# Twenty weight slots for the experts instead of sixteen: constants parted by their life, the normed buffer as a slot

## The reference, cut to what matters

```python
x  = first_block(...)                                   # two layers, RMS norms, feed-forward
h  = rms_norm(x, norm_mix_2);  p = h @ w_in_2           # RWKV, pool, attention, gates
x  = x + (sum of gated branches) @ w_out_2
h  = rms_norm(x, norm_ffn_2)
aff = softmax(h @ router)                               # 256 tokens x 16 experts
for e in experts:                                       # each takes the 32 tokens with the highest affinity
    xe = h[chosen]                                      # 32 x 1024
    ye = (silu(xe @ gate[e]) * (xe @ up[e])) @ down[e]  # three 1024 x 1024 matrices
    x[chosen] += aff[chosen, e] * ye
out = rms_norm(x, norm_final_2)
```

## Time and profile before

| | us |
|---|---|
| median of 3 runs (lowest, highest) | 1851.73 (1849.95, 1852.37) |
| the profiled execution, whole | 1851.07 |
| its span, first to last instruction | 1849.3 |
| PE busy in it | 1551.8 (84%) |
| DMA in the chain that ended last | 25% of the span |
| mean granted PE clock, as a share of full | 0.918 |

### The profile page before, as it was taken

How to read it: one execution, slowest core, us unless ns; L and a number is a source line. 1 busy time by engine, 2 the same in 40 slices (tenths; PEclk the granted TensorE clock), 3 DMA queues, 4 the chain that set the end, 5 groups by cost and what they waited for, 6 DMA issues and landing times.

```text
span 1849.3 us, 25541 instructions
## 1 busy us (share of the span) xinstructions
PE 1551.8 (84%) x11252; PEld 1156.7 (63%) x11252; DVE 539.2 (29%) x1181; ACT 263.1 (14%) x634; POOL 72.1 (4%) x96
## 2 busy tenths in 40 slices
PE   7979999998968999999878778999888666676664
PEld 4857788886736888887756556777774323232221
DVE  3671444402032311005564674422321000000001
ACT  2331100002122100001222232222010000000001
POOL 0230000000000000000011000300000000000000
PEclk8999999998969999999989899999999877878778
DMA  8466577744334544433300000232559999999997
GB/s 369 158 248 271 197 301 298 293 162 153 143 116 158 228 149 147 160 136 117 133 25 2 24 24 2 91 114 91 212 205 404 419 420 420 420 419 420 420 420 291
DMA packets 57630, 405.93 MB, mean 220 GB/s; under 512 B 6184, under 2 KB 8360, under 8 KB 9008
## 3 DMA queue, kind: packets, MB, share of 16 engines
q1 hardware_dynamic: 53696, 388.26, 53.5%
q10 hardware_dynamic: 3824, 16.04, 2.2%
HBM read 403.21 MB, written 1.06 MB: 219 GB/s over the span
## 4 chain that ended last, share of the span: by engine, by line
PE 63%; DMA 25%; DVE 8%; ACT 2%; issue 1%; SPq 0%; POOL 0%; ACTq 0%; DVEq 0%
PE bank L437 62%; DMA weight_ring<-weights 14%; DMA arena<-weights 11%; DVE arena L1567 3%; DVE arena L1573 2%; PE bank L444 1%; ACT arena L1200 1%; DVE arena L1570 1%; DVE arena L1898 1%; DVE rstd L1623 0%; DMA arena<-x 0%; DVE rstd L1965 0%; DVE arena L1760 0%; DVE arena L1896 0%; ACT normed_T L1200 0%
## 5 line engine op out<-in xcount | busy, mean ns | idle before, releaser
L437 PE MATMUL bank<-normed_T,weight_ring 128*128 128x256 f32 x2640 | 607.2, 387 | 27.1 <-ACT arena L1200 12.4
L437 PEld LDWEIGHTS bank<-normed_T,weight_ring 128*128 128x128 f32 x2640 | 503.1, 193 | 108.4 <-ACT arena L1200 18.1
L437 PE MATMUL bank<-arena 64*64 64x64 f32 (+5 forms) x4592 | 340.4, 335 | 82.6 <-DMA arena<-weights 54.0
L437 PEld LDWEIGHTS bank<-arena 64*64 64x64 f32 (+5 forms) x4592 | 223.1, 148 | 207.7 <-DMA arena<-weights 80.3
L437 PE MATMUL bank<-arena,weight_ring 128*128 128x256 f32 x1456 | 329.7, 384 | 9.7 <-ACT arena L1200 6.8
L437 PEld LDWEIGHTS bank<-arena,weight_ring 128*128 128x128 f32 x1456 | 278.3, 192 | 51.0 <-issue 8.5
L1200 ACT ACTIVATE arena<-bank 128x256 f32<-128x256 f32 (+4 forms) x305 | 111.8, 374 | 1130.2 <-PE bank L437 761.7
L1573 DVE SCALAR_TENSOR_TENSOR arena<-arena,bank 128x256 f32<-128x256 f32 x141 | 59.4, 421 | 532.0 <-PE bank L437 275.7
L437 PE MATMUL bank<-weight_ring,arena 128*32 128x256 f32 (+1 forms) x1184 | 108.4, 464 | 61.8 <-DMA weight_ring<-weights 59.7
L437 PEld LDWEIGHTS bank<-weight_ring,arena 128*32 128x32 f32 (+1 forms) x1184 | 41.7, 127 | 123.4 <-DMA weight_ring<-weights 86.0
L444 PE MATMUL bank<-packed_consts,arena 128*128 128x128 f32 (+1 forms) x166 | 42.0, 353 | 61.4 <-DVE arena L1570 27.8
(11 more groups left out here) (130 smaller groups left out, 648.4 us busy)
## 6 DMA issues: line engine op xcount, KB each, us to landing
weight_ring<-weights SPq DMA_DIRECT2D x258, 1024.0 KB, 6.2
arena<-weights SPq DMA_DIRECT2D x88, 1024.0 KB, 27.3
packed_consts<-weights SPq DMA_DIRECT2D x22, 1024.0 KB, 26.4
arena<-weights ACTq DMA_DIRECT2D x8, 1024.0 KB, 18.4
packed_consts<-packed ACTq DMA_DIRECT2D x1, 2848.0 KB
arena<-bias_by_distance ACTq DMA_DIRECT2D x2, 1024.0 KB, 6.9
packed_consts<-weights ACTq DMA_DIRECT2D x2, 1024.0 KB, 35.1
arena<-x SPq DMA_DIRECT2D x1, 1024.0 KB, 5.2
```

Source lines behind the costliest of these rows:

```text
L437: return e.matmul(out, lhsT, rhs, start=start, stop=stop, skip_group_check=True)
```

## The change

- The slots for experts become 20: 14 outside the ring (`EXTRA` = 9 + 3 + 2) and the 6 of the ring. By turn: 0 to 8 are free when the ten were (`AHEAD` = 9); 9 to 11 lie over what the branches use (`BEHIND_BRANCH`); 12 to 17 are the ring; 18 lies over the merged branches, which `w_out_2` reads, and 19 is `hT_` (`BEHIND_W_OUT`).
- ACT issues 14 loads instead of 10: nine at the old place, three more behind a new wait for the last merged branch (`merged`), one behind the eight squares, one behind the four copies to `htok`. SP issues turns 12 to 17 and all from chunk 20 on.
- The constants are parted: 256 late columns stay in `packed_consts`, 5440 columns (`passing`) move to the end of the arena, where slots lie over them later. The late load is now two DMAs.
- `silu_c_copies`, `modulation_rows` and `rstd` become one buffer, in which `final_gain` is loaded; `y_stat` gets a buffer of its own.
- To make room for semaphores, the two of `bias_in` become one (the first attention step waits for both loads), and four of the RWKV's last norm become one, `ln_sum`, counted in the order in which PE raises them.

```diff
-IN_ARENA, IN_CONSTS = 8, 2
-AHEAD = IN_ARENA + IN_CONSTS
+AHEAD = 9
+BEHIND_BRANCH, BEHIND_W_OUT = 3, 2
+EXTRA = AHEAD + BEHIND_BRANCH + BEHIND_W_OUT
...
-        turn = (c - FIRST_EXPERT) % (AHEAD + SLOTS)
+        turn = (c - FIRST_EXPERT) % (EXTRA + SLOTS)
         if c < FIRST_EXPERT:
             slot = c % SLOTS
-        elif turn < AHEAD:
+        elif turn < AHEAD + BEHIND_BRANCH:
             slot = SLOTS + turn
+        elif turn < AHEAD + BEHIND_BRANCH + SLOTS:
+            slot = (FIRST_EXPERT + turn - AHEAD - BEHIND_BRANCH) % SLOTS
         else:
-            slot = (FIRST_EXPERT + turn - AHEAD) % SLOTS
+            slot = turn
...
-    e.dma_start(m.pk[:, EARLY_COLS:NCOLS], dram["packed"][:, EARLY_COLS:NCOLS]).then_inc(s.late, 16)
+    e.dma_start(m.pk[:, EARLY_COLS:KEPT_COLS], dram["packed"][:, EARLY_COLS:KEPT_COLS]).then_inc(s.late, 16)
+    e.dma_start(m.passing, dram["packed"][:, KEPT_COLS:NCOLS]).then_inc(s.late, 16)
...
     e.wait_ge(s.branch_sum, 2 * KD)
     e.wait_ge(s.o_out, 2 * n_items)
-    for c in range(FIRST_EXPERT, FIRST_EXPERT + AHEAD):
-        slot = PLACES[c][0]
-        e.dma_start(m.slots[slot], dram["weights"][c]).then_inc(s.filled[slot], 16)
+
+    def load(*turns):
+        for turn in turns:
+            slot = PLACES[FIRST_EXPERT + turn][0]
+            e.dma_start(m.slots[slot], dram["weights"][FIRST_EXPERT + turn]).then_inc(s.filled[slot], 16)
+
+    load(*range(AHEAD))
+    e.wait_ge(s.merged, KD)
+    load(*range(AHEAD, AHEAD + BEHIND_BRANCH))
     for n in range(KD):
         e.wait_ge(s.xT, 8 * NORM_FFN2 + n + 1)
         act(m.sq8[:, n * T:(n + 1) * T], xT[:, n, :], ACT.Square).then_inc(s.square, 1)
         if n == 0:
             e.preload_act_table(ACT.Sqrt)
+    load(AHEAD + BEHIND_BRANCH + SLOTS)
...
             act(m.htok[:, j, q * 512:(q + 1) * 512], B[2 * j + q][:, :], ACT.Copy, scale=m.st[:, j:j + 1]).then_inc(s.h_tok, 1)
+    load(AHEAD + BEHIND_BRANCH + SLOTS + 1)
...
-            if hd == 0:
-                e.wait_ge(s.bias_in[j], 16)
+            if i == 0:
+                e.wait_ge(s.bias_in, 16 * NT)
...
-        if FIRST_EXPERT <= c < FIRST_EXPERT + AHEAD:
+        if c >= FIRST_EXPERT and c < FIRST_EXPERT + EXTRA + SLOTS and slot >= SLOTS:
             continue
```

More of the change, by code:

```diff
@@ L76, in columns @@
         ("a0", 2 * KR), ("k_k", KR), ("k_a", KR), ("r_k", KR), ("ln_w", KR), ("ln_b", KR), ("pool_scale", KR),
-        ("q_norm", 1), ("k_norm", 1), ("norm_ffn_2", KD), ("rel_bias", HEADS),
+        ("q_norm", 1), ("k_norm", 1), ("norm_ffn_2", KD), ("rel_bias", HEADS), ("router", KD * EXPERTS), ("iota", CAP),
+    ]
+    passing = [
         ("w2", RW), ("a2", RW), ("g2", RW), ("pool_w", 4 * P), ("cos", T), ("sin", T), ("inv_cnt", 4 * T), ("onehot", 2 * T),
-        ("router", KD * EXPERTS), ("iota", CAP), ("blk", P), ("pair", P), ("half", P),
+        ("blk", P), ("pair", P), ("half", P),
         ("strict", 2 * P), ("incl", 2 * P), ("level", LEVELS * HALF), ("eye", HALF),
@@ L82, in columns @@
     at, out = 0, {}
-    for name, n in early + late:
+    for name, n in early + late + passing:
         out[name] = (at, n)
         at += n
-    return out, at, sum(n for _, n in early)
-COLS, NCOLS, EARLY_COLS = columns()
+    return out, at, sum(n for _, n in early), sum(n for _, n in early + late)
+COLS, NCOLS, EARLY_COLS, KEPT_COLS = columns()
 NTILES = (112 * KD + 20 * KD + LRU_HEADS * 8 + KD * KL + 2 * (2 * KF * KD + KD * KF) + 2 * KV_HEADS * KD + HEADS * KD
@@ L179 @@
 REL = {"sum": 1, "row": 2}
-LATE = {"consts": 16, "bias_out": 32, "final_gain": 48}
+LATE = {"consts": 32, "bias_out": 48, "final_gain": 64}
+LN_SUM = {"mean": 1, "var": 2, "bonus": 3, "g": 4}
 ROUTE_PE = {"sum": 2, "aff": 3, "place": 4}
@@ L194, in __init__ @@
             "consts", "late", "x_in", "stored", "freed", "freed_v")]
-        self.bias_in = [sem(f"bias_in{j}") for j in range(NT)]
-        self.filled = [sem(f"filled{j}") for j in range(SLOTS + AHEAD)]
+        self.bias_in = sem("bias_in")
+        self.filled = [sem(f"filled{j}") for j in range(SLOTS + EXTRA)]
         self.v_link, self.a_link, self.g_link, self.zeroed = [sem(n) for n in ("v_link", "a_link", "g_link", "zeroed")]
@@ L230, in __init__ @@
         (self.gram_c, self.masked_c, self.r_sum, self.r_out, self.u_sum, self.u_out, self.s_sum, self.state, self.y_sum, self.y_out,
-         self.mean_sum, self.y_sq, self.var_sum, self.bonus_in, self.bonus_sum, self.bonus, self.ln_root, self.g_sum, self.rwkv_out) = [sem(n) for n in (
+         self.ln_sum, self.y_sq, self.bonus_in, self.bonus, self.ln_root, self.rwkv_out) = [sem(n) for n in (
             "gram_c", "masked_c", "r_sum", "r_out", "u_sum", "u_out", "s_sum", "state", "y_sum", "y_out",
-            "mean_sum", "y_sq", "var_sum", "bonus_in", "bonus_sum", "bonus", "ln_root", "g_sum", "rwkv_out")]
+            "ln_sum", "y_sq", "bonus_in", "bonus", "ln_root", "rwkv_out")]
         (self.qk_pe, self.qk_v, self.qk_a, self.pooled, self.pool_sum, self.yb, self.merged) = [sem(n) for n in (
@@ L269, in __init__ @@
         self.ring = sbuf("weight_ring", SLOTS * TPC * P)
-        self.pk = sbuf("packed_consts", NCOLS)
+        self.pk = sbuf("packed_consts", KEPT_COLS)
         self.xT_ = sbuf("residual_T", KD * T)
@@ L275, in __init__ @@
         self.silu_c = sbuf("silu_c", KD)
-        self.silu32 = sbuf("silu_c_copies", 32 * KD)
-        self.mod_rows = sbuf("modulation_rows", 512)
-        self.rstd = sbuf("rstd", T)
+        rows = sbuf("silu_c_copies_modulation_rows_rstd", D)
+        self.silu32, self.mod_rows, self.rstd, self.final_gain = rows[:, 0:T], rows[:, T:3 * T], rows[:, 3 * T:4 * T], rows[:, :]
+        self.y_stat = sbuf("sums_of_the_last_norm", 5 * NT)
         self.rstd_x = sbuf("rstd_of_the_residual", T)
         n = (nc.sbuf_bytes_remaining // 4 - 64) if not callable(nc.sbuf_bytes_remaining) else nc.sbuf_bytes_remaining() // 4 - 64
+        whole = sbuf("arena", n)
+        self.passing = whole[:, n - (NCOLS - KEPT_COLS):n]
+        n_slot = TPC * P
+        ends = [n - j * n_slot for j in range(EXTRA)]
+        n -= NCOLS - KEPT_COLS
         self.n = n
-        self.area = area = sbuf("arena", n)
+        self.area = area = whole
         self.B = [ctx.enter_context(nc.psum_tensor(f"bank{b}", [P, 512], F32)) for b in range(8)]
@@ L338, in __init__ @@
         self.gates = [a.take(T), self.mod_rows[:, 0:T], self.mod_rows[:, T:2 * T], self.silu32[:, :], self.stage[0][:, 0:T], self.stage[1][:, 0:T]]
-        self.ahead_at = a.at - T - IN_ARENA * TPC * P
         assert a.at <= n - 2 * TW
+        gate0 = a.at - T
         for j in range(24 - N_EARLY):
@@ L343, in __init__ @@
         keep += (24 - N_EARLY) * T
-        n_slot = TPC * P
-        consts = COLS["w2"][0]
         self.slots = [self.ring[:, j * n_slot:(j + 1) * n_slot] for j in range(SLOTS)]
-        self.slots += [area[:, self.ahead_at + j * n_slot:self.ahead_at + (j + 1) * n_slot] for j in range(IN_ARENA)]
-        self.slots += [self.pk[:, consts + j * n_slot:consts + (j + 1) * n_slot] for j in range(IN_CONSTS)]
-        assert consts + IN_CONSTS * n_slot == COLS["router"][0]
+        at = [end - n_slot for end in ends[:-1]]
+        free = [x for x in at if x >= n or x + n_slot <= gate0 and x >= keep + (KD + 2) * T]
+        last = [x for x in at if x < keep + KD * T]
+        branch = [x for x in at if x not in free + last]
+        assert (len(free), len(branch), len(last)) == (AHEAD, BEHIND_BRANCH, BEHIND_W_OUT - 1), (free, branch, last)
+        self.slots += [whole[:, x:x + n_slot] for x in free + branch + last] + [self.hT_[:, :]]
+        self.experts_end = min(at)
         a = Arena(area, n, keep)
@@ L361, in __init__ @@
         self.pbuf2, self.ptb2, self.stat2 = [[a.take(k) for _ in range(NBUF)] for k in (T, NT * P, 4)]
-        a = Arena(self.hT_, KD * T)
-        self.final_gain, self.y_stat = a.take(D), a.take(5 * NT)
         self.yg = self.xT_
@@ L377, in __init__ @@
         self.zeros = a.take(P)
-        assert a.at <= self.ahead_at
+        assert a.at <= self.experts_end
         a = Arena(area, n, a.at)
@@ L382, in __init__ @@
         self.act_, self.hid_e, self.hidT, self.ye, self.comb = [a.take(T) for _ in range(5)]
-        assert a.at <= self.ahead_at
+        assert a.at <= self.experts_end
     def col(self, name, j=0, n=1):
         a = COLS[name][0] + j
+        if a >= KEPT_COLS:
+            return self.passing[:, a - KEPT_COLS:a - KEPT_COLS + n]
         return self.pk[:, a:a + n]
@@ L885, in finish @@
         e.wait_ge(s.y_out, 4 * ct + 4)
-        mm(B[4][:, 0:T], m.blk, m.yaT[:, ct * T:(ct + 1) * T], True, True).then_inc(s.mean_sum, 1)
+        mm(B[4][:, 0:T], m.blk, m.yaT[:, ct * T:(ct + 1) * T], True, True).then_inc(s.ln_sum, 1)
         yield
         e.wait_ge(s.y_sq, ct + 1)
-        mm(B[4][:, 0:T], m.blk, m.y2, True, True).then_inc(s.var_sum, 1)
+        mm(B[4][:, 0:T], m.blk, m.y2, True, True).then_inc(s.ln_sum, 1)
         e.wait_ge(s.bonus_in, ct + 1)
```

(14 more changed lines are left out.)

## The result

The changed kernel took 1842.02 us in the median of five runs (1838.19 to 1843.18), beside 1851.37 us (1849.59 to 1852.37) for the kernel before: ratio 0.9943, 95% interval 0.993 to 0.9957. Beside other kernels, on chips of their own sessions, it was measured twice more: 0.9945 (0.9933 to 0.9957) and 0.9937 (0.9922 to 0.9951). The forecast was 1841.6 us. Between these two medians lie 9.4 us.

The account below looks back on a forecast made before the run. The kernel's end was taken as bound by a constant-rate weight stream starting at the first freed slot. Four chunks at 2.517 us save 10.1 us, other parts zero: 1851.73 - 10.1 = 1841.6 us, forecast range 1840.0 to 1843.2.

Parts of the forecast that it names:

- The four slots: Expert weight stream: 19 chunks loaded ahead instead of 15, each worth 2.517 us; gain 10.1 us, bounds 10.0 and 10.2.
- The room in the gap: Idle DMA stretch before the experts, 1364.9 to 1386.0 us: all four added loads in before 1386 us, 6 us to spare.
- some 2 MB: Sign to check: the strip's slice around 1364 to 1386 us, before the experts, carries some 2 MB more.
- Turn 19: ACT's load behind the last copy to htok, starting at 1374.4 us, landed by some 1380 us.
- ACT's issues: ACT behind the merged wait: three issues, 1.5 us, done at 1337.1 us before the first square at 1338.5; cost nothing.
- The rival of a queue that blocks: ACT's three issues behind merged blocked 6.58 us each, PE standing 14.1 us: 1855.7 us; chance 0.05.
- Late constants, semaphores, addresses: Split late load bounded by 2 us gain or loss, taken as zero; merged semaphores and moved buffers cost nothing.
- The end: Last 16 matmuls take 1.07 us in full clock, 1.93 in half: 0 to +0.9 us, 1 us allowed in all.
- The check points: Last landing 1827.4 us instead of 1837.5; stream rate stays 420 GB/s; first waited landing later than 1412 us.

Follow-up runs that it names:

- another megabyte: Changed kernel with the 0.5 MB final_gain load done twice more, before the first expert; 1838.98 us beside 1838.43 for the changed kernel, ratio 0.9938 to the kernel before.
- Sixteen slots: Changed kernel with four slots taken away, all its other parts kept; 1849.59 us beside 1850.69 for the kernel before, ratio 0.9994.
- the kernel with two late slots: Changed kernel, all twenty slots, but turns 18 and 19 loaded only beside final_gain, as the first expert is about to start; ratio 0.9964 to the kernel before.
- pair of zeros and the freed slot: Changed kernel with the last w_out_2 slot freed in route_sums and two matmuls of zeros per late chunk of the last expert; ratio 0.9945 to the kernel before.
- eighteen: Changed kernel without ACT's two late routing loads (turns 18 and 19); ratio 0.9973 to the kernel before, stream 446.5 us.

## Why the prediction was right

*The four slots.* Foretold 10.1 us; the stream fell by 10.3 us in the first profile, and by 9.9 us from sixteen to twenty slots (451.2 to 441.3). The pace in the changed kernel is (1826.82 - 1428.73) / 158 chunks = 2.520 us, against 2.517 before. From the two kernels between, a stored chunk is worth (451.2 - 446.5) / 2 = 2.35 us and (446.5 - 441.3) / 2 = 2.6 us. By the share of HBM that "DMA: Bandwidth & Descriptors" of the Trainium skill gives (section "Bandwidth") it would be 2.9 us. The prediction set that share against the measurement without its condition: the same section gives it for two cores of a pair that both stream, and 425 GB/s for loads of 16 MB by a core alone. The runs, with one core at work, show 420 GB/s, so they are against the share and not against the page.

*The room in the gap.* Right: 150 GB/s in it, and with another megabyte in it still no cost. The gap carried 3.1 MB more and not "some 2 MB": of the two chunks more that were to pass ahead of it, only one had by 1364.6 us, and the other ran on until 1367 us, where the prediction itself has the queues run empty. Turn 19 came at 1371.0 us and not at 1374.4 us. That issue stands 0.6 us ahead of the four copies that precede it in the program (1371.65 us), as turn 18's stands at the start of the eighth square and not at its end. The step was too cautious.

*ACT's issues.* Right: 0.33 to 0.72 us each, the three behind the merge done at 1336.6 us (forecast 1337.1), and the first square didn't wait. The rival of a queue that blocks didn't come true.

*Late constants, semaphores, addresses.* Taken at zero with 2 us to either side. Sixteen slots with all of them gave 0.9994 (0.9985 to 1.0003), so zero stands, with 2.8 us at most of a gain. In the first profile the stage around 124 us stood 1.9 us later than before, which looked like a loss; by 568 us it was gone. The profiles scatter here anyway: one landmark, a table load on ACT, stands at 565.07 us in the kernel with two late slots, at 568.35 us before, at 568.11 us in the changed kernel and at 570.49 us with the pair of zeros and the freed slot, while from there to the table load of the routing these four take 801.5 to 801.7 us. In order: before, changed, two filled late, pair of zeros and freed slot:

```profile
568.35 1.28 ACT L1223 ACT_TABLE_LOAD   x1
1369.97 1.28 ACT L1512 ACT_TABLE_LOAD   x1
```

```profile
568.11 1.28 ACT L1237 ACT_TABLE_LOAD   x1
1369.66 1.28 ACT L1534 ACT_TABLE_LOAD   x1
```

```profile
565.07 1.28 ACT L1237 ACT_TABLE_LOAD   x1
1366.70 1.28 ACT L1533 ACT_TABLE_LOAD   x1
```

```profile
570.49 1.28 ACT L1244 ACT_TABLE_LOAD   x1
1372.13 1.28 ACT L1541 ACT_TABLE_LOAD   x1
```

*The end.* I named the right thing and sized it too small: 0.9 us for the last 16 matmuls, 1 us in all. It is 1.8 us, since the second group of 16 is slower too (2.11 against 1.17 us). In the profiled run this is why the span fell by 8.9 us and not by 10.1 us; that the median came out within 0.4 us of the forecast has some luck in it: the medians differ by 9.4 us and not by 10.1, and the forecast started from a median before of 1851.73 us where the kernel before, timed beside the changed one, had 1851.37 us.

*The check points.* The last landing was forecast for 1827.4 us and came at 1826.8 us; the rate stayed at 420 GB/s; the first waited landing moved from 1412 to 1428.7 us.

## What to carry to other kernels

Where a kernel ends in a stream at the rate of its DMA engines, its end is the time of the first load of the stream plus the bytes still to come: look for a stretch ahead of it in which the engines are idle, count the chunks that could be stored there, and each is worth its bytes over the rate and no more. Ask of each slot when it is really freed, too: here a signal that waited for the next weight matmul kept one slot empty for 17 us. To judge a change of a few us, cut the profile at landmarks (start, stream, tail); the changed kernel's stream repeated to 1.2 us in three profiles, where its runs scattered by 5 to 7 us.

## What the runs showed that was not expected

- The tail has two lengths, 11.8 and 13.6 us, by PE's clock at the last chunk, at the same work. In the kernel with sixteen slots it was the half clock, with eighteen the full; the table shows no order in it.
- An added matmul of a 128x128 by a 128x512 tile in float32 takes 1.0 to 1.1 us in the full clock and appears as two in the trace. Two per chunk made PE the bound of the last expert (stream +2.2 us), one per chunk didn't.
- The sixteen DMA engines don't finish the stream together: in its last 11 us their mean share is 0.40 to 0.65 in the twelve profiles that are bound by landings to the end. Much of what a stream is longer or shorter by than its bytes say, 1 to 2 us, lies there.
- Much of the scatter between profiles arises before 568 us, where they differ by up to 5.4 us; from there to the routing thirteen of the fourteen profiles take 801.5 to 801.7 us, and one (the changed kernel's third) 799.9 us.
